# Routed experts in blocks of token rows: one block shared by two neighbouring experts

## The reference, cut to what matters

```python
grp = jnp.argmax(coarse_logits, axis=-1)
top_v, top_i = lax.top_k(fine_sel, 2)
expert_idx = grp[:, None] * 8 + top_i
for e in range(32):                      # w_gate, w_up: 1024 x 256, w_down: 256 x 1024
    hid = silu(t @ w_gate[e]) * (t @ w_up[e])
    out = out + combine[:, e:e+1] * (hid @ w_down[e])
```

```
13 11 106 69 | 11 73 6 153 | 25 27 36 45 | 7 14 6 6 | 1 6 7 70 | 20 66 17 29 | 67 21 28 49 | 71 27 6 59
```

## Time and profile before

| | |
|---|---|
| time before, median of 3 runs | 630.71 us (628.97 to 632.04) |
| the profiled execution | 630.07 us, of which its span 628.3 us |
| expert stage, first gate_up to last down | 312.86 to 590.43 us |
| blocks | 41 |
| PE, DVE, ACT, POOL busy over the span | 87%, 46%, 20%, 37% |
| HBM read over the span | 133.2 MB |

### The profile page before, as it was taken

The page is one execution under the profiler, slowest core; times in us unless marked ns, Lnnn a source line. Parts: engine busy times, 40 slices in busy tenths (PEclk is TensorE's granted clock), DMA queues, the critical chain, the costliest instruction groups (busy, mean ns, idle before and its releaser), DMA issues.

```text
span 628.3 us, 10982 instructions
## 1 busy us (share of the span) xinstructions
PE 548.8 (87%) x3508; PEld 327.1 (52%) x3509; DVE 291.1 (46%) x621; ACT 128.6 (20%) x250; POOL 230.4 (37%) x362
## 2 busy tenths in 40 slices
PE   5969999999929999994889999999999999999500
PEld 2657777777717445543445554554544554554200
DVE  3307999999984324447522222222222222222174
ACT  5201000000104221112112212222212222222243
POOL 2001111745712401225324444444444544545344
PEclk9598999999968999995999999999999999999955
DMA  8993006000000792009469998899999999998193
GB/s 252 318 365 135 2 0 268 1 2 0 1 0 0 248 422 116 33 35 387 179 235 319 315 338 321 283 358 399 350 371 376 361 390 340 357 390 281 28 332 117
DMA packets 37331, 141.72 MB, mean 226 GB/s; under 512 B 10200, under 2 KB 14304, under 8 KB 25017
## 3 DMA queue, kind: packets, MB, share of 16 engines
q1 hardware_dynamic: 25786, 127.75, 55.2%
q0 software_dynamic: 4736, 9.45, 4.8%
q10 hardware_dynamic: 6783, 4.16, 2.2%
HBM read 133.22 MB, written 12.52 MB: 232 GB/s over the span
## 4 chain that ended last, share of the span: by engine, by line
PE 57%; issue 15%; DVE 12%; ACTq 4%; DMA 3%; ACT 3%; DVEq 2%; SPq 1%; POOL 1%; POOLq 0%
PE bank L1296 25%; PE bank L1312 12%; PE bank L1193 8%; PE bank L1288 4%; DVE z L859 4%; ACTq L472 3%; DVE region_h L1070 2%; DVE z L855 2%; PE bank L1318 2%; DMA region_x<-in_x_sample 2%; PE bank L1131 1%; PE bank L1217 1%; ACTq L474 1%; PE bank L1252 1%; DVEq L859 1%
## 5 line engine op out<-in xcount | busy, mean ns | idle before, releaser
L1131 PE MATMUL bank<-region_h,region_w 128*128 128x288 f32 x640 | 162.9, 419 | 6.1 <-ACT region_x L467 5.1
L1131 PEld LDWEIGHTS bank<-region_h,region_w 128*128 128x128 f32 x640 | 125.7, 197 | 42.3 <-issue 5.6
L855 DVE SCALAR_TENSOR_TENSOR z<-ub,par,z x120 | 91.9, 766 | 0.0
L1296 PE MATMUL bank<-region_w,z 128*64 128x256 f32 x704 | 84.6, 391 | 2.0 <-issue 2.0
L1044 DVE TENSOR_TENSOR ua<-ua,bank 128x128 f32<-128x128 f32 x41 | 11.8, 289 | 152.4 <-ACT ua L573 152.4
L714 POOL DMA_INDIRECT region_x<-h_rows,gcol x44 | 58.1, 1321 | 62.2 <-issue 61.3
L1296 PEld LDWEIGHTS bank<-region_w,z 128*64 128x64 f32 x704 | 48.3, 134 | 30.7 <-issue 2.3
L1039 DVE COPY sb_rows<-region_x 64x1024 f32<-64x1024 f32 x43 | 47.6, 1108 | 35.8 <-DMA region_x<-h_rows,gcol 32.9
L751 POOL DMA_INDIRECT y_rows<-ua,scol x41 | 40.2, 981 | 56.0 <-issue 56.0
L1193 PE MATMUL bank<-region_w,z 128*128 128x512 f32 x128 | 56.8, 597 | 1.4 <-POOL z L695 1.0
L1312 PE MATMUL bank<-region_w,ua 128*32 128x512 f32 x448 | 53.9, 598 | 0.5 <-ACT ua L580 0.5
(11 more groups left out here) (211 smaller groups left out, 554.6 us busy)
## 6 DMA issues: line engine op xcount, KB each, us to landing
region_w<-in_w_down SPq DMA_DIRECT2D x21, 1024.0 KB, 6.2
region_w<-in_w_gate SPq DMA_DIRECT2D x16, 1024.0 KB, 6.6
region_w<-in_w_up SPq DMA_DIRECT2D x16, 1024.0 KB, 6.6
region_w<-in_w_in SPq DMA_DIRECT2D x3, 2048.0 KB, 20.8
slot<-in_w_gate SPq DMA_DIRECT2D x6, 1024.0 KB, 6.1
slot<-in_w_up SPq DMA_DIRECT2D x6, 1024.0 KB, 6.8
slot<-in_w_down SPq DMA_DIRECT2D x6, 1024.0 KB, 5.8
region_x<-in_w_up SPq DMA_DIRECT2D x5, 1024.0 KB, 7.1
```

The costliest lines, as they stand in the source:

```text
L855: nc.vector.scalar_tensor_tensor(out=zc[:, 0:SEQ], in0=up, scalar=pc[:, j:j + 1], in1=zc[:, 0:SEQ], op0=ALU.mult, op1=ALU.add).then_inc(s_ ...
L1131: ins = mm(ps[2 * bank + j][:, 0:HALF], sec[name][:, k, c * P:(c + 1) * P], hT[:, k, j * HALF:(j + 1) * HALF], start=(k == 0), stop=(k == ...
L1296: ins = mm(ps[1][h * T:(h + 1) * T, 0:2 * P].rearrange("p (w f) -> p w f", w=2), xT[:, k, :], wgu[i][:, :, k, h, :], start=(k == 0), stop= ...
```

## The change

Experts 2m and 2m+1 share one block: rows 0 to 31 hold up to 32 tokens of the even one, rows 32 to 63 up to 32 of the odd one. What an expert has beyond 32 tokens fills blocks of its own with 64 rows: the even one's stand before the shared block, the odd one's behind it. With c tokens an expert has ceil((c-32)/64) own blocks, or none. By the counts above that is 16 shared blocks and 14 own, 30 in all. In order of the pairs, own blocks of the even one and of the odd one:

```diff
-NBLK = NE + (2 * NTOK - 1) // T
+NPAIR = NE // 2
+NBLK = NPAIR + NE + (2 * NTOK - NE * (T // 2 + 1)) // T
...
-                size = pool.value_load(big[0:1, bass.ds(g, 1)], min_val=0, max_val=2)
-                with pool.If(size > 1):
-                    fetch(b, T)
...
+                fetch(b)
...
+                link(nc.vector.tensor_scalar(two(pari, t), vi[:, 0:2], 1, None, ALU.bitwise_and))
+                nc.vector.tensor_scalar(two(low32, t), two(pari, t), -float(T // 2), float(T // 2), ALU.mult, ALU.add)
+                nc.vector.tensor_scalar(two(sgn, t), two(pari, t), 2.0, -1.0, ALU.mult, ALU.add)
...
-                link(nc.vector.tensor_copy(two(ranki, t), two(rankf, t)))
+                link(shifted(t))
                 link(split(t))
-                nc.vector.tensor_copy(two(rplf, t), two(rpl, t)).then_inc(s_place, 1)
+                link(halve(t))
+                placed(t).then_inc(s_place, 1)
...
-                    ins = place_rows(nc.vector, NT - 1)
+                    ins = placed(NT - 1)
...
-            link(nc.vector.tensor_tensor(sbase, last, nbi[:, 16:16 + NE], ALU.subtract))
-            link(nc.vector.tensor_tensor(ohe, ohe, sbase.unsqueeze(1).to_broadcast([P, 2 * NT, NE]), ALU.mult))
+            for i in range(2 * NT):
+                ins = nc.vector.tensor_tensor(ohp[:, i * NPAIR:(i + 1) * NPAIR, :], ohp[:, i * NPAIR:(i + 1) * NPAIR, :],
+                                              shared.to_broadcast([P, NPAIR, 2]), ALU.mult)
...
+            place_rows(nc.vector, NT - 1).then_inc(s_placel, 1)
...
-            for m, row in zip(more, (T, T // 2)):
-                nc.vector.tensor_scalar(m[0:1, :], vtok[row:row + 1, :], float(2 * NTOK), None, ALU.is_lt)
...
                 nc.vector.tensor_tensor(hid, sg_m, ps[1][:, P:2 * P], ALU.mult).then_inc(s_hid, 1)
-                move(q + 1, b)
                 dve.wait_ge(s_hT_ps, q * 2 + (b + 1))
                 nc.vector.tensor_copy(hidT, ps[2][:, 0:P]).then_inc(s_hidT, 1)
+                move(q + 1, b)
...
+                        for half, i in enumerate(halves):
+                            r0 = h * T + half * H
+                            ins = mm(ps[1][r0:r0 + H, 0:2 * P].rearrange("p (w f) -> p w f", w=2),
+                                     xT[:, k, half * H:(half + 1) * H],
+                                     wgu[i][:, :, k, h, :], start=(k == 0), stop=(k == KC - 1))
                 ins.then_inc(s_gu, 1)
                 pe.wait_ge(s_mv, g + 2)
                 mm(ps[5][0:32, 0:1], onesb[:, 0:32], onesb[:, 0:1], start=True, stop=True)
+                tokens(0, KC // 2)
                 pe.wait_ge(s_hid, g + 1)
                 tr(ps[2][:, 0:P], hid, ident[:, :]).then_inc(s_hT_ps, 1)
+                tokens(KC // 2, KC).then_inc(s_xt_ps, 1)
+
+                pe.wait_ge(s_hidT, g + 1)
+                pe.wait_ge(s_yc, g + 1)
...
+            def pair(it, i):
...
+                for part in range(2):
+                    pe.wait_ge(s_wexp[i][part], it * 16 + 16)
+                with pe.If(after > first + 1):
+                    with pe.Fori(first, after - 1) as g:
+                        block_of(g, (i, i), it)
+                for part in range(2):
+                    pe.wait_ge(s_wexp[i + 1][part], it * 16 + 16)
+                block_of(after - 1, (i, i + 1), it)
+                with pe.If(end > after):
+                    with pe.Fori(after, end) as g:
+                        block_of(g, (i + 1, i + 1), it)
```

More of the change, by code:

```diff
@@ L583, in _ @@
             tokens_out(1)
[L584 to L589, removed]
-                for b in range(2):
[L591 to L596, removed]
-            with act.If(odd > 0):
[L598 to L602, removed]
+            for b in range(2):
+                block_of(0, b)
+            with act.Fori(1, pairs) as q:
+                for b in range(2):
+                    block_of(q, b)
+            with act.If(odd > 0):
+                block_of(pairs, 0)
             nc.scalar.activation(small[:, 62:63], eps_rms, ACT.Sqrt)
@@ L746, in scatter @@
                 pool.tensor_tensor(carry[:, 2:3], carry[:, 1:2], carry[:, 1:2], ALU.add)
[L748 to L753, removed]
+                pool.indirect_dma_start(y_half, bass.IndirectOffsetOnAxis(ap=scol[:, b:b + 1], axis=0),
+                                        yblk[b], None,
+                                        bounds_check=4 * NTOK - 1, oob_is_err=False).then_inc(s_ysc[b], 16)
             for g in range(2, 4):
@@ L932, in split, with shifted, halve, placed @@
                 return nc.vector.tensor_scalar(two(rpl, t), two(ranki, t), T - 1, None, ALU.bitwise_and)
+            def shifted(t):
+                return nc.vector.tensor_scalar(two(ranki, t), two(rankf, t), float(T // 2), None, ALU.add)
+            def halve(t):
+                nc.vector.tensor_tensor(two(sgnq, t), two(qrel, t), two(sgn, t), ALU.mult)
+                return nc.vector.scalar_tensor_tensor(out=two(lower, t), in0=two(qrel, t), scalar=0.0, in1=two(low32, t),
+                                                      op0=ALU.is_equal, op1=ALU.mult)
+            def placed(t):
+                return nc.vector.tensor_tensor(two(rplf, t), two(rpl, t), two(lower, t), ALU.subtract)
             def place(t):
@@ L1284, in _, with tokens, block_of @@
             wdn = [w.rearrange("p (c d) -> p c d", c=F // P) for w in slot_dn]
-            def tokens():
-                for k in range(KC):
+            H = T // 2
+            def tokens(k0, k1):
+                for k in range(k0, k1):
                     ins = tr(ps[0][:, k * T:(k + 1) * T], xrow[:, k * P:(k + 1) * P], ident[0:T, 0:T])
-                ins.then_inc(s_xt_ps, 1)
-            def gate_up(i, g):
+                return ins
+            def block_of(g, halves, turn):
                 pe.wait_ge(s_xt, g + 1)
@@ L1322, in _ @@
             pe.wait_ge(s_mv, 1)
-            tokens()
-            def expert(it, i):
-                first = pe.value_load(bound[0:1, bass.ds(it * NSLOT + i, 1)], min_val=0, max_val=NBLK - 1)
-                end = pe.value_load(bound[0:1, bass.ds(it * NSLOT + i + 1, 1)], min_val=1, max_val=NBLK)
-                pe.wait_ge(s_wexp[i][0], it * 16 + 16)
-                pe.wait_ge(s_wexp[i][1], it * 16 + 16)
-                gate_up(i, first)
-                if i:
-                    down(i - 1, first)
-                elif isinstance(it, int):
-                    down(NSLOT - 1, first)
-                else:
-                    with pe.If(it > 0):
-                        down(NSLOT - 1, first)
-                pe.wait_ge(s_wexp[i][2], it * 16 + 16)
-                hid_transpose(first)
-                with pe.If(end > first + 1):
-                    with pe.Fori(first + 1, end) as g:
-                        gate_up(i, g)
-                        down(i, g)
-                        hid_transpose(g)
@@ L1348, in _ @@
-            with pe.Fori(0, NE // NSLOT) as it:
-                for i in range(NSLOT):
-                    expert(it, i)
-            for i in range(NE % NSLOT):
-                expert(NE // NSLOT, i)
-            nblk = pe.value_load(bound[0:1, NE:NE + 1], min_val=NE, max_val=NBLK)
-            down((NE - 1) % NSLOT, nblk)
+            tokens(0, KC).then_inc(s_xt_ps, 1)
+            def pair(it, i):
+                e = it * NSLOT + i
+                first = pe.value_load(bound[0:1, bass.ds(e, 1)], min_val=0, max_val=NBLK - 1)
+                after = pe.value_load(bound[0:1, bass.ds(e + 1, 1)], min_val=1, max_val=NBLK)
+                end = pe.value_load(bound[0:1, bass.ds(e + 2, 1)], min_val=1, max_val=NBLK)
+                for part in range(2):
[9 more added lines that the diff above has]
+                        block_of(g, (i + 1, i + 1), it)
@@ L1358 @@
+            with pe.Fori(0, NE // NSLOT) as it:
+                for i in range(0, NSLOT, 2):
+                    pair(it, i)
+            for i in range(0, NE % NSLOT, 2):
+                pair(NE // NSLOT, i)
 _INS = ["x_prompt", "x_sample", "state_conv_a", "state_conv_b", "g_mix", "w_in", "conv_a_w", "conv_b_w",
```

87 lines of the change are left out of this document (46 added, 41 removed).

## The result

The changed kernel takes 638.72 us (median of 20 runs, 631.14 to 653.69) against 631.25 for the kernel before (20 runs, 628.19 to 637.97). The ratio is 1.0083, with a 95% interval from 1.0054 to 1.0112, so it is slower, by some 5 us. Forecast were 623.0 us and a range of 614 to 634. Medians here and in the tables are over all executions, ratios over those with undisturbed clocks alone, and as the execution profiled first (653.69 us) was disturbed, the profile shown here is that of a second set of runs of the same kernel (`after_again`, 639.28 us, span 637.5).

A forecast was written before the change was run, and what follows sets the result against it. PE bounds the stage's first 106 us, PE and transfers neck and neck the last 152; afterwards transfers bind. Stage -7.9, routing -0.4, end +0.8 sum to -7.5 on 630.07: 622.6, as median 623 us; range 614 to 634.

The forecast's parts named there:

- The stage, by the transfers: Expert stage: weight slots come free earlier, transfers set the pace, last `down` ends at 582.5 against 590.4, a gain of 7.9.
- the new padding costs no bytes: Gathers and scatters of the expert stage: rows without a token move nothing, so transfers stay at not more than 90.2 MB.
- Rival B: Expert stage: nothing won, early DMA share stays 0.89 as pairs free two slots at once and late; 631 us, chance 0.2.
- C: Shared gate_up: its four matmul groups do not run side by side; 648 us at the upper bound, chance 0.1.
- D: Expert blocks: stalls, loops and a low clock make PE's blocks grow; 652 us at 10 us a block, chance 0.05.
- Around the stage: Routing before the stage and the end after it: -0.4 for the size tables gone, +0.8 for a later last scatter.
- The four groups: Shared block's gate_up: 64 matmuls of 32 columns run side by side, 3.84 us plus 0.2, bounds +0 and +3.84.
- Order and loops in a block: Each block: waiting for its own product makes 7.15 us (+0.5), uncovered loops and branches add 0.65; 7.8 in all.
- The clock: PE's clock drops after waits for weights; only the last pair pays, 1 us taken.
- The end: After the last `down`: DVE's later copy delays the last scatter about 1.2, less 0.4 for the lookup, +0.8.
- Rival E: Expert stage: more is won, with 7.2 us blocks and transfers at 373 GB/s throughout; 615 us, chance 0.15.

The follow-up runs named there:

- a_spread: Changed kernel with neighbouring tokens of an expert placed four rows apart in their half block, by index patterns only; 627.92 us, 0.9924 of the kernel before.
- a_65_spread: Changed kernel with the inversion tile 65 columns wide again and neighbouring tokens four rows apart; 629.41 us, 0.9947 of the kernel before.
- a_65: Changed kernel with the inversion tile 65 columns wide again, as before the change, in place of 64; 634.74 us, 1.0036 of the kernel before.

## Why the prediction was wrong

**The step that failed is "The stage, by the transfers".** It took 98 engine-busy us and 3.6 idle for ten experts, 101.6 us, and 9.26 us for each later one, from rows in which gathers had 16, 32 or 64 rows by need. The runs showed 111.67 us and 9.67. In the early stretch the engines were busy for 0.92 of it, 102.7 us, at 320 GB/s (318 before), and idle for 9. The forecast needed the slack of that stretch (share 0.89) to fill up once PE freed slots sooner. Slots did come sooner, SP's waits on PE fell from 36.9 to 9.5 us, and the slack stayed. Behind it stands the sentence "the new padding costs no bytes": true, but where the tokens stand in the padding costs time, and so do the full sizes. The size lookups, which the diff takes away, were booked as a relief for GpSimd alone.

What the runs put in its place has three parts. The place of the tokens: `a_spread` brings the early stretch back to 100.63 us, as forecast, and the time down by 9.8 us. Two parts under way: a third one is worth 13 us with neighbouring rows and 18 with spread ones. The full sizes: in the old blocks they cost the late stretch 7 to 8 us, and the changed kernel ran it 6.2 us late; that these 6.2 are theirs is likely and was not tried. The two stretches ran 16.3 us late, of which spreading took back 13.6 in `a_spread` and 8.5 in `a_65_spread` against `a_65`. Why the place matters is open as far as the skew is only argued.

**Rival B came nearest, for another reason.** It expected 631 us with the 0.89 kept because pairs free slots late. The 0.89 was nearly kept, but by transfers waiting for transfers. Its price was 8 us too low. Its other half, a late rate of 9.26 us an expert, was too good as well (9.67). C and D, which held the chance of slower, did not happen.

**The step "Around the stage" was wrong in sign at its front.** I had -0.4 for the routing's end; expert 6 came 4.2 us late. The last inversion matmul starts at 305.80 in place of 303.20, 2.6 us: the 40 matmuls, which I took to last as long as before, take 5.5 us in place of 1.4, less 1.4 us because the first of them starts sooner (300.55 for 301.97). From there to the first gate_up it is 11.24 us in place of 9.66, another 1.6, with 1.91 us of idle PE on issue just ahead of it: the loops and branches of the first pair, which I had priced for every block but not here.

**The four groups: right.** A shared gate_up takes 3.7 to 3.9 us (I had 3.84 + 0.2, bounds +0 and +3.84), and each matmul lasts 424 ns on average (424 to 457 by buffer), not a turn for each pair. Of the rule in "TensorE: Matmul & The Clock Gate", Part 3, of the Trainium skill, that loads of equal row groups don't overlap, the trace shows the opposite: 49.44 us of loads in 110 us of which PE is busy for 97.67, and a gate_up as short as with two groups.

**Order and loops in a block: right in sum.** Where PE doesn't wait for weights, a block takes 7.0 to 7.1 us inside a pair (I had 7.15 before control work) and 8.3 to 9.0 when it is the last of its pair, with 1.2 to 1.8 us idle on issue. I had 7.8 for all, bounds 7.2 and 8.9. PE's sum stayed far below the transfers'.

**The clock: right in kind, small.** 0.85 and 0.80 in the late windows held nothing up that shows: a gate_up after a long wait took up to 6.5 us in place of 3.84, but SP never waited for PE there. The last shared gate_up ran at 0.69 and took 5.38 us instead of 3.8, so 1.6 where I had 1. From its start (586.1) to the end of `down` (601.94) it is 15.8 us, against 16.0 forecast.

**The end: too dear.** I had +0.8. From the last `down` to the first load of `y_rows` it is 5.08 us against 5.35. After that the same work takes 30.5 us to the end of the span against 32.5, and so in the other kernels with the new blocks (30.5 to 31.2) and with the old ones (32.1 to 32.4). This 2 us was not looked into.

**Rival E: not reached.** It needed 373 GB/s throughout the stage; the changed kernel had 333, and the best of its variants 381 at a share of 1.00. The 425 GB/s of the Trainium skill, "HBM Reference", stand there under Specifications (TRN2), not under Access. The changed kernel came near them only ahead of the stage, with 416 GB/s from 296 to 300 us, where weights are loaded and nothing is gathered.

**The sum.** 4.4 + 10.1 + 6.2 is 20.7 us late for expert 31, 19.4 at the last `down`, and the cheaper end gives 2.7 back: 622.6 + 19.4 - 2.7 = 639.3, the profiled execution's 639.28.

## What to carry to other kernels

When an edit unloads the engine that bounds a stage, read first what the transfers can do by themselves: a share of 0.9 with the queue waiting on transfers alone means that too few are under way, or that something loads the engines unevenly, and no slot freed earlier will help. An indirect transfer that skips most of its rows is not free padding; place the live rows apart, or keep its row count near what is live. Here the idea paid 2.7%, and it stayed hidden until a third part was under way (1.5%) and the rows were spread.

## What the runs showed of the hardware

- Where a token stands in a block is worth 1.55% (0.93 to 0.97 of the engines, 333 to 355 GB/s), with bytes and instructions unchanged.
- Alternating weight tiles of 128 and 64 columns, small matmuls start every 135 ns; alternating 128 and 65, every 29 ns.
- Full-size gathers and scatters with most rows empty slow the transfers: fifteen experts' weights take 147.12 us and 145.75 with spread rows, against 138.95 with sizes by need.
- Gathers of 4.7 MB cost 30 to 35 us. Beside them, weight packets ran at 365 GB/s, without them at 383, and with them at 384 where rows were spread and three parts under way.
- With spread rows and three or four parts, the stage ran at 377 and 381 GB/s at a share of 1.00. The same share of 0.99 had meant 359 with neighbouring rows.
